# Accumulating scatter of a mixture-of-experts layer in two column halves, with GpSimd's loop written out

## What is computed

```python
def run_block(args):
    tok, wrow, e = args
    xb = x_pad[tok]
    hb = jax.nn.silu(xb @ we_gate[e]) * (xb @ we_up[e])
    return (hb @ we_down[e]).astype(jnp.float32) * wrow[:, None]
...
routed = jnp.zeros((n_tok + 1, dm), jnp.float32).at[row_tok].add(
    y_rows.reshape(n_rows, dm))[:n_tok]
shared = (jax.nn.silu(xt @ ws_gate) * (xt @ ws_up)) @ ws_down
return (routed.astype(x.dtype) + shared).reshape(bsz, seq, dm)
```

## Time and profile before

| what | us |
|---|---|
| median of three runs | 1501.82 |
| the three runs | 1500.01, 1501.82, 1502.33 |
| span of the profiled execution | 1500.0 |
| stages up to the router | about 703 |
| shared expert and first gate and up | 703 to 753 |
| blocks 0 to 64, first scatter to last landing | 753 to 1467 |
| last layer norm and output | 1467 to 1500 |

### The profile page before, as it was taken

One profiled execution on the slowest core, in us unless ns is written; L12 is line 12 of the kernel. 1 busy time (PEld: TensorE's weight loads), 2 busy tenths in 40 slices (PEclk: granted clock), 3 DMA queues, 4 the chain that ended last, 5 costly groups with the idle time before them and its releaser, 6 DMA issues.

```text
span 1500.0 us, 17023 instructions
## 1 busy us (share of the span) xinstructions
PE 1397.8 (93%) x5222; PEld 714.7 (48%) x5222; DVE 796.5 (53%) x1420; ACT 368.4 (25%) x737; POOL 613.9 (41%) x590
## 2 busy tenths in 40 slices
PE   7999999999997999998999999999999999999970
PEld 4444666666664455553444444444444444444430
DVE  3576999999986248892433333333333334333326
ACT  0324656566554122210010101001001001001015
POOL 0009444555500003352345555555555455455520
PEclk9999999999999999999999999999999999999995
DMA  9406110010135601062699999999999999999946
GB/s 236 80 28 75 19 20 13 14 19 17 38 101 193 226 15 43 29 239 92 257 330 376 364 371 369 348 366 368 363 373 364 343 375 364 371 375 349 327 101 237
DMA packets 116408, 322.15 MB, mean 215 GB/s; under 512 B 46470, under 2 KB 66590, under 8 KB 91394
## 3 DMA queue, kind: packets, MB, share of 16 engines
q1 hardware_dynamic: 92946, 261.99, 47.8%
q0 software_dynamic: 23408, 59.45, 16.3%
HBM read 276.45 MB, written 51.72 MB: 219 GB/s over the span
## 4 chain that ended last, share of the span: by engine, by line
DMA 41%; PE 5%; issue 4%; DVE 2%; POOLq 1%; ACT 0%; POOL 0%; ACTq 0%; SPq 0%
DMA sum_d<-moe_y,moe_idx 40%; PE moe_p_gu L1716 2%; PE moe_p_s L1752 2%; PE moe_p_y L1736 1%; DVE all_x_sb L1930 1%; DVE all_x_sb L1925 1%; DMA moe_xg<-x_d,moe_idx 1%; DMA all_x_sb<-sum_d 0%; POOLq L1658 0%; POOL moe_xg L1662 0%; POOL sum_d L1673 0%; POOLq L1699 0%; ACT moe_junk L1832 0%; DVE moe_y L1864 0%; POOLq L1659 0%
## 5 line engine op out<-in xcount | busy, mean ns | idle before, releaser
L1847 DVE STREAM_TRANSPOSE moe_xgT<-moe_xg 128x1024 f32<-128x1024 f32 x65 | 132.0, 2031 | 418.0 <-DMA moe_xg<-x_d,moe_idx 418.0
L1662 POOL DMA_INDIRECT moe_xg<-x_d,moe_idx x260 | 264.5, 1017 | 115.9 <-issue 59.7
L1736 PE MATMUL moe_p_y<-mixers_ring_b,moe_hT 128*128 128x512 f32 x520 | 233.9, 592 | 1.0 <-DVE moe_hT L1858 1.0
L1716 PE MATMUL moe_p_gu<-mixers_ring_b,moe_xgT 128*128 128x512 f32 x512 | 225.0, 592 | 0.0
L1673 POOL DMA_INDIRECT sum_d<-moe_y,moe_idx x65 | 105.7, 1627 | 244.3 <-DMA sum_d<-moe_y,moe_idx 207.1
L1784 ACT ACTIVATE moe_sig<-moe_p_gu 128x256 f32<-128x256 f32 x65 | 25.0, 385 | 586.9 <-PE moe_p_gu L1716 586.9
L1736 PEld LDWEIGHTS moe_p_y<-mixers_ring_b,moe_hT 128*128 128x128 f32 x520 | 98.7, 190 | 125.0 <-issue 123.9
L1716 PEld LDWEIGHTS moe_p_gu<-mixers_ring_b,moe_xgT 128*128 128x128 f32 x512 | 95.1, 191 | 107.1 <-issue 107.1
L1242 POOL DMA_INDIRECT slot_d<-all_entry,all_dest_i x48 | 48.5, 1010 | 221.1 <-DVE all_dest_i L1488 209.0
L717 PE MATMUL att_p_s<-latents_kT,att_qT 128*128 128x512 f32 x256 | 123.5, 605 | 0.7 <-ACT att_v_last L892 0.7
L1716 PE MATMUL moe_p_gu<-mixers_ring_a,moe_xgT 128*128 128x512 f32 x272 | 119.5, 592 | 0.0
(11 more groups left out here) (324 smaller groups left out, 1923.5 us busy)
## 6 DMA issues: line engine op xcount, KB each, us to landing
mixers_ring_b<-in_we_down_dram SPq DMA_DIRECT2D x65, 1024.0 KB, 8.8
mixers_ring_b<-in_we_gate_dram SPq DMA_DIRECT2D x32, 1024.0 KB, 10.2
mixers_ring_b<-in_we_up_dram SPq DMA_DIRECT2D x32, 1024.0 KB, 15.7
mixers_ring_a<-in_we_gate_dram SPq DMA_DIRECT2D x17, 1024.0 KB, 9.7
mixers_ring_a<-in_we_up_dram SPq DMA_DIRECT2D x17, 1024.0 KB, 14.9
mixers_o<-in_we_gate_dram SPq DMA_DIRECT2D x16, 1024.0 KB, 10.1
mixers_o<-in_we_up_dram SPq DMA_DIRECT2D x16, 1024.0 KB, 15.5
moe_xg<-x_d,moe_idx POOLq DMA_INDIRECT x260, 6.9
```

The source lines that it names most:

```text
L1662: nc.gpsimd.indirect_dma_start(xg[:, u, g, :], None, x1_quarters, bass.IndirectOffsetOnAxis(ap=idx[:, c, g:g + 1], axis=0), bounds_check=N ...
L1716: last = nc.tensor.matmul(p_gu[:, u, :], xgT[:, u, kk, :], k.moe_gu[v][:, :, kk * F:(kk + 1) * F], start=(kk == 0), stop=(kk == KD - 1))
L1736: last = nc.tensor.matmul(p_y[:, half * 512:(half + 1) * 512], hT[:, u, kk, :], k.moe_dn[v][:, kk * D + half * 512:kk * D + (half + 1) * 512],
L1847: nc.vector.transpose(xgT[:, u].rearrange("p k (g i) -> p g k i", g=NQ), xg[:, u].rearrange("p g (j k) -> p g k j", k=KD)).then_inc(x_turn ...
```

## The change

Three things are changed together.

- The scatter of a block becomes two, one for each half of the columns. `sum_d` is seen as rows of 512 floats, two for each token, and the slot table gets a sixth column: the two scatter indices of a slot are 2 x token and 2 x token + 1. The half of columns 0 to 511 waits for `y_act` only and for its own predecessor's landing (`y_out[0]`), the other half for `y_dve` and `y_out[1]`. ACT and DVE wait for the half that they write.
- GpSimd's loop over blocks is written out, so that a transfer takes its indices straight from the slot table. The copy at L1658 and the wait behind it are gone for the 65 blocks that this run has.
- In the table's making one DVE operation on 112 columns becomes two.

```diff
-            ch.link(nc.vector.tensor_copy(k.block_idx[:, :, NQ], p_x[:, NQ, 0:COLS]))
+            for half in range(2):
+                ch.link(nc.vector.tensor_scalar(k.block_idx[:, :, NQ + half], p_x[:, NQ, 0:COLS], 2.0, float(half), ALU.mult, ALU.add))
...
-        idx = sb("idx", [P, 6, NQ + 1], i32)
+        idx = sb("idx", [P, 2, NQ + 2], i32)
+        sum_halves = k.sum_d.rearrange("n (h w) -> (n h) w", h=2)
...
-        y_out = sem("y_out")
+        y_out = [sem(f"y_out{half}") for half in range(2)]
...
-            def gather(n, col, u, c, free=None):
-
+            def gather(at, u, free=None):
                 if free is not None:
                     pool.wait_ge(x_turned, free)
-                nc.gpsimd.tensor_copy(idx[:, c, :], k.block_idx[:, bass.ds(col, 1), :].rearrange("p b g -> p (b g)")).then_inc(idx_done, 1)
-                pool.wait_ge(idx_done, n + 1)
                 pool.sem_inc(idx_seen, 1)
                 for g in range(NQ):
                     nc.gpsimd.indirect_dma_start(xg[:, u, g, :], None, x1_quarters,
-                                                 bass.IndirectOffsetOnAxis(ap=idx[:, c, g:g + 1], axis=0),
+                                                 bass.IndirectOffsetOnAxis(ap=at[:, g:g + 1], axis=0),
                                                  bounds_check=NQ * SEQ - 1, oob_is_err=False).then_inc(xg_in[u], 16)
 
-            def scatter(n, u, c, first=False):
-
-                pool.wait_ge(y_act, n + 1)
-                pool.wait_ge(y_dve, n + 1)
-                if not first:
-                    pool.wait_ge(y_out, n * 16)
-                pool.sem_inc(y_taken, 1)
-                nc.gpsimd.indirect_dma_start(k.sum_d[:, :], bass.IndirectOffsetOnAxis(ap=idx[:, c, NQ:NQ + 1], axis=0),
-                                             y[:, u, :], None, compute_op=ALU.add).then_inc(y_out, 16)
+            def scatter(n, at, u, first=False):
+                for half, made in enumerate((y_act, y_dve)):
+                    pool.wait_ge(made, n + 1)
+                    if not first:
+                        pool.wait_ge(y_out[half], n * 16)
+                    pool.sem_inc(y_taken, 1)
+                    nc.gpsimd.indirect_dma_start(sum_halves, bass.IndirectOffsetOnAxis(ap=at[:, NQ + half:NQ + half + 1], axis=0),
+                                                 y[:, u, half * 512:(half + 1) * 512], None, compute_op=ALU.add).then_inc(y_out[half], 16)
+
+            def block_of(n):
+                return k.block_idx[:, OVER + n if n < E else 0, :]
...
             pool.wait_ge(sum_out, 16 * T)
...
+            for n in range(E + 1):
+                scatter(n, block_of(n), n % 2, first=(n == 0))
+                if n + 4 <= E:
+                    gather(block_of(n + 4), n % 2, free=n + 3)
...
-                    act.wait_ge(y_out, e * 16 - 16)
+                    act.wait_ge(y_out[0], e * 16 - 16)
...
-                    dve.wait_ge(y_out, e * 16 - 16)
+                    dve.wait_ge(y_out[1], e * 16 - 16)
```

33 lines of the change are left out of this document (12 added, 21 removed).

## The result

The changed kernel takes **1510.77 us** (median of 4 runs, 1508.81 to 1514.8); the kernel before, on the same chip, 1502.07 us (4 runs, 1500.01 to 1503.67). The ratio is 1.006, with a 95% interval of 1.0043 to 1.0076: slower by 9 us, where I forecast 1492, faster by 10. The time lies in the stated range, but on the other side of no change.

What follows compares the result with a forecast made beforehand. Scatter chain and full DMA engines were taken to bound the block stage side by side. Table +0.4, block stage -7.7 and tail -2 gave -9.3 us from 1501.8, so 1492, with range 1480 to 1515.

Steps and rivals of the forecast that it cites:

- What bounds the kernel now: Block stage: scatter chain at 11.18 us a block beside DMA engines needing about 11.25; TensorE needs 10.53.
- 16 blocks at 10.53 us: Block stage: TensorE's pace holds until the weights' 17.0 us of room is used up, saving 10.6 us.
- The scatter's wait: Scatter chain: a half flies 8 us, plus 0.8 is under 10.53, so the chain no longer binds.
- rival B: No change: a half flies as long as the whole, or small second-transfer costs eat the gain; 1502 us, chance 0.15.
- DMA work of two halves: DMA engines, block stage: same bytes, two 2 KB rows share one packet, so 0 added; otherwise 0.13 us a block.
- Rival C: Slower: the second accumulate costs DMA time in the block stage, deciding from 0.16 us a block; 1521 us, chance 0.21.
- Two issues: GpSimd: each half's issue takes 1.6 us; GpSimd needs 9.0 us a block, under 10.53.
- The index copy: GpSimd, ahead of gathers: removal frees 1.6 us a block inside the scatter wait, giving nothing by itself.
- The tail: End of span: last scatter lands about 1466.7 after waiting for its predecessor; halves of 5 us give some 2 us.
- The fixed cost of a transfer: Per DMA, about 2 us: agrees as latency with a 6.2 us landing; as DMA time, 116 us more, contradicted by rows.
- The table: DVE, slot table's making: one operation of 0.36 us becomes two, +0.4 us on the path.
- Rival A: Block stage: TensorE's pace all through, the 37.7 us come nearly whole; 1462 us, chance 0.10.

Runs made afterwards that it cites:

- e9: Kernel before, whole scatter, with up weights not reloaded after the first ring (stale ones used): 1467.66 us, ratio 0.9772.
- e14: Changed kernel with whole scatters, going alternately to two sums, each waiting for the one before the last: 1491.31 us, ratio 0.9925.
- e3: Changed kernel with halves by rows (64 rows of 4 KB each), the second into a sum of its own: 1495.76 us, ratio 0.996.
- e16: The changed kernel run once more, unaltered: 1512.21 us, ratio 1.0058 against the kernel before.
- e4: Changed kernel with each weight transfer cut into two with rows of 4 KB: 1515.65 us, ratio 1.01 against the kernel before.
- e13: Changed kernel with column halves going alternately to two sums, each waiting for the half two blocks back: 1505.7 us, ratio 1.0013.
- e5: Kernel before, whole scatter, with each weight transfer cut into two with rows of 4 KB: 1508.42 us, ratio 1.0039.
- e15: Changed kernel with the scatter made whole again, GpSimd's program still written out, a repeated run: 1508.29 us, ratio 1.0037 against the kernel before.
- e8: Changed kernel with weights loaded for only 64 of 128 partitions from the fifth expert on: 1536.79 us, ratio 1.0205.
- e6: Kernel before, whole scatter, with a bounds check so that a block's empty rows are skipped: 1513.77 us, ratio 1.0081.
- e11: Kernel before, whole scatter, empty rows skipped and each block's rows spread over the partitions: 1488.2 us, ratio 0.9903.

## Why the prediction was wrong

**What bounds the kernel now** was read rightly. Two bounds lie side by side, and the change loosens one: e9 shows TensorE's pace once DMA has room, e14 that with the chain gone the lead of the weights is spent and the rest is the DMA's pace. Two sizes were off. "16 blocks at 10.53 us" was short: e14 and e3 have next to no gap in TensorE's work until 980, some 23 blocks. And the DMA's pace is 11.13 to 11.16 us, not 11.25. By both e14's block stage is 11.1 us shorter than before's, where the sum says 7.7. That e14's median of 1491.31 meets my 1492 is partly luck: it gained 13.1 us, not 9.3, and the runs of the kernel before beside it had a median of 1504.44, not 1501.8.

**"The scatter's wait" is the step that failed.** I took 8 us for a half's flight from a range of 5 to 10.3, arguing that less to move takes less time. It measured 10.5 us (e16), above the 10.3 us of a whole one, which I had called the most it could be. That is rival B, and its mechanism (halves share their queue with gathers, and the engines with weights) is what e3 and e4 show: a half flies for 7.8 to 8.8 us when it has half the packets, or when the weights' packets are half as long. Rival B's time, 1502, was still too low. The last step of a landing is the late one: in e16 half of the 16 steps are there after 8.8 to 9.0 us (8.8 in before), and in e14 all lie between 9.9 and 10.4. What holds the last ones back in the kernels that wait for them is not shown. The condition, that flight plus 0.8 us be under 10.53, wasn't met: 10.5 + 0.8 = 11.3, and the changed kernel's steps are 11.2 to 11.4.

**"DMA work of two halves" failed with it.** I took 0, since two rows of 2 KB should be one packet. They are not. q0 has 143 packets more a block, about the 128 of one more row each, and 16 for one more transfer. I had priced this case: 0.13 us a block from the 12-byte rows, 7.5 us in all (58 x 0.136 is 7.9). By the shares of q0, and above, it is 34.8/104.2 x 11.25 = 3.76 us a block instead of 3.61: 0.15 us. As DMA work the bound was right and the choice between the ends wrong, but this work isn't what costs time: the pace of e13's last 40 blocks is that of before. The price is in waiting. A row that is its own packet is one more packet between which the weight queue can put one of its own. e4 halves the length of those and frees the chain, e13 keeps them and stays slow though no scatter waits for the one before it. Rival C put the cost in the DMA engines' pace, at 0.16 us a block or more, and its time at 1521; the changed kernel's last 40 blocks are 0.06 us a block slower than before's.

The Trainium skill (DMA: Bandwidth & Descriptors, Queues, rings and completion order) says that an engine goes round its queue rows packet by packet. e3, e4, e5 and e13 agree with it. An estimate from packet times fits as well: with a weight packet of 0.31 to 0.32 us ahead of each of its own, an engine's eight 4 KB packets (0.327 us) take 5.1 us; halving the weight packets takes 1.2 us off (measured: 10.3 to 9.2), having four packets in place of eight 2.6 (measured: 10.3 to 7.8). It is tempting to go further and count which queue ends last: q0 has 479 packets a block beside 19232/44.4 = 433 of weights in the changed kernel, 336 beside 433 before, and 851 stand beside it in e4. But 122 of the 479 have 4 or 16 bytes, and without such small ones it is some 357 beside 385. So that q0 ends last because it has more packets is not shown.

**Two issues** cost what was said: 1.6 us each, and GpSimd had the time.

**The index copy** gave nothing by its removal, as said. But the written-out program that came with it, costed at nothing, cost 4 us (e15), copy removed and all. I named instruction loading as a sign to look for and put no price on it.

**The tail** was read wrongly. I took its end, 1466.7, for the landing of the last scatter and forecast -2. The last scatter had landed at 1466.2; the end is GpSimd's walk through the loop of absent blocks behind the last issue, and it grew: by 1.4 us in the span behind the blocks. A half's flight without weights is 5.9 us, where I had 5. From DVE's last weighting to the last issue it is 3.0 us instead of 3.5, all that is left of my 2.

**The fixed cost of a transfer.** I wrote that the landing of 6.2 us agrees with the Trainium skill's 2 us beside the bytes. By those figures half a megabyte takes 3.2 us, an estimate; only the direction agrees. That it isn't DMA time is borne out by e3: its 65 further transfers make its block stage 0.7 us longer than e14's.

**The table** is +0.4 us, as said. **Rival A**, TensorE's pace all through, happened nowhere with the weights loaded in full.

Put together by the measured terms, against before's profile: table +0.4; block stage +5.3 instead of -7.7; behind it +1.4 instead of -2: +7.1 us, beside a median that rose by 8.7. The rest is not accounted for.

## What to carry to other kernels

Beside full DMA engines the flight of a scatter here followed how many packets it had and how long the other queue's were, far more than its bytes: splitting it by columns makes more packets of shorter rows and lands no sooner (10.5 us, whole 10.3), while splitting it by rows keeps the packets and does (7.8, from three full records, and 8.7). When one of two queues has a lead to spend, an edit that makes the other one late forfeits it: that, and not more DMA work, was 13.5 us between e13 and e14. When two bounds lie within a few per cent, look for the edit that lowers the shared one (here rows spread over the partitions and empty ones skipped, 1% faster) before the edit that takes a wait out of the other. A program written out wasn't free against a loop (+3.9 us in e15, cause open), and behind the last piece of work every branch still walked is on the path.

## What the runs showed of the hardware

- A row of 2 KB in an indirect accumulate is a packet of its own: 21264 packets for 41.20 MB, against 15047 for 41.59 MB with rows of 4 KB. Of the 21264, 11379 have 2048 bytes; the gathers' rows of 1 KB travel in packets of 4096. Median times: 176 ns for 2 KB added, 327 for 4 KB added, 159 for 4 KB gathered.
- Loading 64 of the 128 partitions took 62.1% of the DMA engines' time for 67 MB (e8), loading all of them 69.4% for 140 MB.
- A scatter of 64 rows of 4 KB landed after 7.8 and 8.7 us (e3), one of 128 rows of 2 KB after 10.6 and 10.5 (e16), one of 128 rows of 4 KB after 10.3 (before).
- Skipped rows on the last partitions freed DMA time (33.1% to 29.6%) and gained no time (e6, ratio 1.0081); spread over the partitions, nearly the same skipping gave 0.9903 (e11).
- The same loop of untaken branches on GpSimd took 0.22 us a round in one program and 0.30 us in another that differs ahead of it.
- Cutting the weights' packets from 8 to 4 KB raised q1's share from 69.4% for 140.03 MB to 70.9% for 137.66 MB, and cut DVE's wait for gathers from 371.7 to 61.9 us (e4).
